# Conv taps read through a DRAM copy of u, and transposes moved from the DMA queues to TensorE, in a hybrid encoder layer

## What is computed

```python
proj = x @ w_in
glu_in, q, k, v, q_mem, gate_logits = split(proj)
a, g = split(glu_in)
u = a * sigmoid(g)                                  # (S, 512)
y_conv = silu(layer_norm(depthwise_conv(u, 31) + dw_b)) @ w_conv_out
y_attn = windowed_gqa(q, k, v, rel_bias, sink) @ w_attn_out   # 8 heads of 64, keys within 128
y_mem = memory_attention(q_mem, mem, w_mem_kv) @ w_mem_out    # 4 heads of 128, 256 keys
gates = sigmoid(gate_logits + b_gate)
merged = gates[0] * y_conv + gates[1] * y_attn + gates[2] * y_mem
x1 = layer_norm(alpha * x + merged @ w_o)
out = layer_norm(alpha * x1 + (silu(x1 @ w_gate) * (x1 @ w_up)) @ w_ffn_out)
```

## Time and profile before

| | |
|---|---|
| three runs | 1162.78, 1255.37, 1316.87 us; median 1255.37 |
| profiled execution | 1163.56 us |
| its slowest core, first to last instruction | 1161.7 us |
| all cores | 1131.6 to 1161.7 us |
| TensorE busy on the slowest core | 1001.5 us (86%) |
| VectorE, ScalarE, GpSimd busy | 403.0, 344.2, 138.0 us |

### The profile page before, as it was taken

The page is one execution under the profiler, slowest core; times in us unless marked ns, Lnnn a source line. Parts: engine busy times, 40 slices in busy tenths (PEclk is TensorE's granted clock), DMA queues, the critical chain, the costliest instruction groups (busy, mean ns, idle before and its releaser), DMA issues.

```text
span 1161.7 us, 15497 instructions; the slowest of 8 cores (1131.6 to 1161.7 us)
## 1 busy us (share of the span) xinstructions
PE 1001.5 (86%) x5526; PEld 456.1 (39%) x5526; DVE 403.0 (35%) x756; ACT 344.2 (30%) x499; POOL 138.0 (12%) x181
## 2 busy tenths in 40 slices
PE   4993995486787399999999874799999999999996
PEld 1441442243333144444444331344444444444442
DVE  1331362352755022222235742334311522251224
ACT  1141563262644022222222463522211211121111
POOL 2200000110113043433330010000000000000000
PEclk9996998897989699999999998899999999999998
DMA  9996112753213689760039599961542144215401
GB/s 136 167 185 107 38 49 62 125 70 74 54 29 59 100 138 180 116 111 1 1 80 277 120 153 131 130 179 55 169 158 91 70 166 152 84 75 179 145 1 72
DMA packets 76042, 124.60 MB, mean 107 GB/s; under 512 B 42240, under 2 KB 52104, under 8 KB 74720
## 3 DMA queue, kind: packets, MB, share of 16 engines
q0 software_dynamic: 13408, 49.55, 24.9%
q1 hardware_dynamic: 45664, 69.87, 21.2%
q10 hardware_dynamic: 16896, 4.20, 5.6%
HBM read 138.32 MB, written 19.93 MB: 136 GB/s over the span
## 4 chain that ended last, share of the span: by engine, by line
PE 71%; DMA 9%; SPq 8%; issue 4%; DVE 3%; ACT 2%; ACTq 1%; POOL 0%; DVEq 0%; POOLq 0%
PE ps L229 71%; SPq L144 7%; DMA arena<-arena 7%; DMA arena<-w_bf_cache 2%; DMA arena<-xt 1%; ACTq L279 1%; DVE arena L1004 1%; DVE arena L1006 1%; ACT arena L1049 1%; SPq L279 1%; DVE arena L589 0%; ACT arena L596 0%; ACT arena L1083 0%; DVE arena L647 0%; DVE arena L675 0%
## 5 line engine op out<-in xcount | busy, mean ns | idle before, releaser
L229 PE MATMUL ps<-arena 128*128 128x512 bf16 (+5 forms) x5372 | 994.7, 368 | 149.5 <-DMA arena<-arena 62.3
L229 PEld LDWEIGHTS ps<-arena 128*128 128x128 bf16 (+2 forms) x5372 | 451.4, 100 | 691.3 <-issue 218.1
L1085 DVE TENSOR_TENSOR arena<-ps,arena 128x512 bf16<-128x512 f32 x88 | 59.7, 690 | 210.1 <-PE ps L229 169.5
L813 DVE SCALAR_TENSOR_TENSOR arena<-arena,ps 128x512 f32<-128x512 f32 x96 | 65.8, 686 | 176.7 <-PE ps L229 172.4
L792 ACT ACTIVATE arena<-ps,bgate_sb 128x512 f32<-128x512 f32 x96 | 65.9, 687 | 189.2 <-PE ps L229 189.2
L1083 ACT ACTIVATE arena<-ps 128x512 f32<-128x512 f32 x88 | 51.3, 597 | 176.4 <-PE ps L229 174.3
L983 ACT ACTIVATE arena<-arena 128x1024 bf16<-128x1024 f32 (+1 forms) x32 | 33.8, 1056 | 152.6 <-DVE arena L1106 128.7
L820 POOL TENSOR_TENSOR arena<-arena 128x512 f32<-128x512 f32 x32 | 41.0, 1283 | 192.7 <-DVE arena L813 192.7
L144 POOL DMA_DIRECT2D out<-arena x16 | 8.5, 532 | 416.3 <-DVE arena L1006 416.3
L644 ACT ACTIVATE arena<-ps 128x1024 bf16<-128x1024 f32 x46 | 46.4, 1023 | 34.1 <-PE ps L229 34.0
L825 POOL TENSOR_TENSOR arena<-arena 128x512 bf16<-128x512 f32 x32 | 40.9, 1277 | 55.9 <-DVE arena L813 48.2
(11 more groups left out here) (81 smaller groups left out, 294.1 us busy)
## 6 DMA issues: line engine op xcount, KB each, us to landing
arena<-w_bf_cache SPq DMA_DIRECT2D x88, 512.0 KB, 3.3
arena<-arena SPq DMA_DIRECT2D x256, 33.8 KB, 1.9
arena<-x SPq DMA_DIRECT2D x16, 512.0 KB, 25.7
out<-arena POOLq DMA_DIRECT2D x16, 512.0 KB, 2.9
arena<-w_f POOLq DMA_DIRECT2D x22, 256.0 KB, 16.3
arena<-w_g POOLq DMA_DIRECT2D x9, 512.0 KB, 12.7
arena<-xt POOLq DMA_DIRECT2D x8, 512.0 KB, 30.5
w_bf_cache<-w_f POOLq DMA_DIRECT2D x8, 512.0 KB, 54.6
```

The costliest lines, as they stand in the source:

```text
L229: return pe.run(lambda: nc.tensor.matmul(out, lhsT, rhs, start=start, stop=stop), deps, inc)
L813: t_y = dve.run(lambda: nc.vector.scalar_tensor_tensor(out=gb[r], in0=gb[r], scalar=1.0, in1=ps[:, bk, :], op0=ALU.add, op1=ALU.mult), [tk ...
L1085: t_a = dve.run(lambda: nc.vector.tensor_tensor(out=actT[:, j, :], in0=ps[:, bU, :], in1=sgf[sr], op=ALU.mult), [tU, t_s, e_state["dep"]])
```

## The change

Three parts. (1) Each piece of u is also stored to DRAM (`u_scratch`) as soon as it exists, on SyncE's queue, and a conv unit's buffer is filled by 4 loads from there, one per shift r, each with 128 runs of 540 elements; the loads wait for the stores of the neighbouring pieces. (2) `w_T` and `m_T` become four TensorE transposes into one single PSUM bank and a copy out of it (VectorE for windowed attention; ScalarE and VectorE in turn, two to one, for memory attention). They are no longer called one piece after the product but are queues `t` and `u` of their own, and `ORDER` is a new string. (3) `d_T` becomes eight TensorE transposes (`d_Tpe`) and a ScalarE copy out of PSUM (`d_Tev`), called two chains later, so that the loop makes two more chains, and the first FFN step stands behind eleven chains instead of ten.

```diff
 ORDER = (
-    "wwawawawkwaawwawawawaawawawwmaacmwacmcmawkmcwawamcwwamcwawawamwcwackcwkcawaccamaakmacaaccmawacaw"
+    "wawawaawwawaaaawawaawwktamwawamwtwwcmwaawuamcwtwkcwakwcmawcmmamcwawawcautwccamcuaacutkwtwawmacmam"
...
+    u_d = nc.dram_tensor("u_scratch", [128, 4, T + 48], BF16, kind="Internal")
...
-    UQ = [[V(143 + 4.25 * i + 1.0625 * j, [128, 544]) for j in range(4)] for i in range(3)]
+    UQr = [V(143 + 4.25 * i, [128, 4, 544]) for i in range(3)]
...
         th_free[r] = [t_u[k, c]]
+        u_store(k, c)
         uq_pump()
...
+    def u_store(k, c):
+        lo = 512 * k + (32 if k else 0)
+        hi = 512 * k + (544 if k < 3 else UW - 512 * 3)
+        ud_tok[k, c] = dma(sp, u_d.ap()[:, c, lo:hi], U0[:, c, lo:hi], ud_slot[4 * k + c], [t_u[k, c], t_pads])
...
     def uq_issue(i):
         k, c = cunits[i]
         r3 = i % 3
-        deps = [t_u[k, c], t_pads, uq_free[r3], btab["st"], btab["cw"]]
-        if k > 0:
-            deps.append(t_u[k - 1, c])
-        if k < 3:
-            deps.append(t_u[k + 1, c])
-        for j in range(4):
-            for r in range(4):
-                lo = 32 + 512 * k - 15 + r
-                uq_tok[i] = dma(sp, UQ[r3][j][32 * r:32 * r + 32, 0:540], U0[32 * j:32 * j + 32, c, lo:lo + 540],
-                                uq_slot[r3], deps)
+        deps = [uq_free[r3], btab["st"], btab["cw"]] + [ud_tok[kk, c] for kk in range(max(k - 1, 0), min(k + 2, 4))]
+        for r in range(4):
+            lo = 32 + 512 * k - 15 + r
+            src = bass.AP(u_d, c * UW + lo, [[4 * UW, 32], [32 * 4 * UW, 4], [1, 540]])
+            uq_tok[i] = dma(sp, UQr[r3][32 * r:32 * r + 32, :, 0:540], src, uq_slot[r3], deps)
...
-    def w_T(n, t_o):
+    def w_T(n):
+        b, dd = banks.alloc(1)
         r = n % 2
-        t_oT[n] = dma_t(sp, qT[:, :, n * 128:(n + 1) * 128], otm[r].rearrange("p a b c -> p (a b c)"), wt_slot[r], [t_o])
-        otm_free[r] = [t_oT[n]]
+        t_o = wst.pop(("V", n))
+        of = otm[r].rearrange("p a b c -> p (a b c)")
+        for c4 in range(4):
+            t_tr = pe.run(lambda: nc.tensor.transpose(
+                psb[:, b, c4 * 128:(c4 + 1) * 128], of[:, c4 * 128:(c4 + 1) * 128], ident_bf[:]),
+                [t_o, dd, t_ident] if c4 == 0 else (), inc=(c4 == 3))
+        otm_free[r] = [t_tr]
+        src = psb[:, b, 0:512].rearrange("p (a b) -> p a b", a=4)
+        t_oT[n] = dve.run(lambda: nc.vector.tensor_copy(qT[:, :, n * 128:(n + 1) * 128], src), [t_tr])
+        banks.release(b, t_oT[n])
...
-    def m_T(u, t_o):
+    def m_T(u):
...
+        om_free[r] = [t_tr]
+        t_omT[u] = evac(qmT[:, h, tt * 512:(tt + 1) * 512], psb[:, b, 0:512], [t_tr])
+        banks.release(b, t_omT[u])
...
-    def d_T(tb):
+    def d_Tpe(tb):
         r = tb % 3
-        t_x1T[tb] = dma_t(act, x1T[:, :, tb * 128:(tb + 1) * 128], x1b[r], xt_slot[r], [d_state.pop(("cb", tb))])
-        x1b_free[r] = [t_x1T[tb]]
+        t_cb = d_state.pop(("cb", tb))
+        bT, dT = banks.alloc(1)
+        for kc in range(8):
+            t_tr = pe.run(lambda: nc.tensor.transpose(
+                psb[:, bT, kc * 128:(kc + 1) * 128], x1b[r][:, kc * 128:(kc + 1) * 128], ident_bf[:]),
+                [t_cb, dT] if kc == 0 else (), inc=(kc == 7))
+        x1b_free[r] = [t_tr]
+        d_state["tr", tb] = (bT, t_tr)
+
+    def d_Tev(tb):
+        bT, t_tr = d_state.pop(("tr", tb))
+        t_x1T[tb] = act.run(lambda: nc.scalar.copy(
+            x1T[:, :, tb * 128:(tb + 1) * 128], psb[:, bT, :].rearrange("p (a b) -> p a b", a=8)), [t_tr])
+        banks.release(bT, t_x1T[tb])
...
+        if 0 <= k - 2 < 16:
+            d_Tpe(k - 2)
         if k + 2 < 16:
             d_S(k + 2)
-        if k >= 0:
+        if 0 <= k - 2 < 16:
+            d_Tev(k - 2)
+        if 0 <= k < 16:
             d_C(k)
...
-        if k >= 0:
-            d_T(k)
...
-    while chain["k"] < 16:
+    while chain["k"] < 16 + 2:
         d_chain()
-        if chain["k"] > 5:
+        if chain["k"] > 6 + 2:
             e_step(si)
```

More of the change, by code:

```diff
@@ L87 @@
 ORDER = (
[L88 to L90 removed]
+    "wawawaawwawaaaawaawawwktamwawamtwwcmwaawuamcwtwkcwakwcmawcmmamcwawawcautwccamcuaacutkwtwawmacmam"
+    "wkuwaccwcacwamckcawwatwctwwacaagwaucwwacccaogmagggkgcmoagacawgmccamtamgagcwoumcucwwcatwumcgacaka"
+    "wgcwmcauccawwacatmacaaawwaawacctcwwcacmctwaccaawaamwamcwaummuaccmactuawaamwacccaaaawaacatwbmauwm"
+    "aamtaauauaaaaaaaa"
 )
@@ L275, in _build @@
     t_small = dma(sp, esink8[:], sinkp_d.partition_broadcast(128).rearrange("p a b -> p (a b)"), s_small)
[L277 to L281, removed]
     def load(out, in_, deps=(), e=None, name="ld"):
@@ L476, in _build @@
     uq_pend = []
+    ud_slot = [new_slot("ud") for _ in range(16)]
+    ud_tok = {}
+    def u_store(k, c):
+        lo = 512 * k + (32 if k else 0)
+        hi = 512 * k + (544 if k < 3 else UW - 512 * 3)
+        ud_tok[k, c] = dma(sp, u_d.ap()[:, c, lo:hi], U0[:, c, lo:hi], ud_slot[4 * k + c], [t_u[k, c], t_pads])
     def uq_load(i):
@@ L653, in w_V @@
         res = wst["S", n]
+        assert otm_free[n % 2] is not None
         b, dd = banks.alloc(2)
@@ L676, in w_V @@
         banks.release(b, t_o, 2)
-        later(1, lambda: w_T(n, t_o))
-    wt_slot = [new_slot("wt") for _ in range(2)]
-    def w_T(n, t_o):
+        wst["V", n] = t_o
+        otm_free[r] = None
+    def w_T(n):
+        b, dd = banks.alloc(1)
         r = n % 2
-        t_oT[n] = dma_t(sp, qT[:, :, n * 128:(n + 1) * 128], otm[r].rearrange("p a b c -> p (a b c)"), wt_slot[r], [t_o])
-        otm_free[r] = [t_oT[n]]
+        t_o = wst.pop(("V", n))
[8 more added lines that the diff above has]
+        banks.release(b, t_oT[n])
     def w_steps(n):
@@ L721, in m_V @@
         t_e = mst.pop(("S", u))
+        assert om_free[r] is not None
         b, dd = banks.alloc(2)
@@ L739, in m_V @@
         banks.release(b, t_o, 2)
-        later(1, lambda: m_T(u, t_o))
-    mt_slot = [new_slot("mt") for _ in range(2)]
-    def m_T(u, t_o):
+        mst["V", u] = t_o
+        om_free[r] = None
+    def m_T(u):
         tt, h = munits[u]
         r = u % 2
-        t_omT[u] = dma_t(sp, qmT[:, h, tt * 512:(tt + 1) * 512].rearrange("p (a b) -> p a b", a=4),
-                         omtm[r].rearrange("p a b -> p (a b)"), mt_slot[r], [t_o])
-        om_free[r] = [t_omT[u]]
+        t_o = mst.pop(("V", u))
+        b, dd = banks.alloc(1)
+        for tbl in range(4):
+            t_tr = pe.run(lambda: nc.tensor.transpose(
+                psb[:, b, tbl * 128:(tbl + 1) * 128], omtm[r][:, tbl, :], ident_bf[:]),
+                [t_o, dd, t_ident] if tbl == 0 else (), inc=(tbl == 3))
+        om_free[r] = [t_tr]
+        t_omT[u] = evac(qmT[:, h, tt * 512:(tt + 1) * 512], psb[:, b, 0:512], [t_tr])
+        banks.release(b, t_omT[u])
     mdn = nc.alloc_sbuf_tensor("mdn", [128, 2, 4], F32)
@@ L911, in _build @@
              qm_list(2) + qm_list(3) + c_main(0, 0) + c_main(0, 1) + c_main(0, 2) + c_main(0, 3))
-    in_order(ORDER, a=mains, w=cat(W), m=cat(M), c=cat(CV), g=[wg_drip(b, i) for b in range(3) for i in range(4)],
+    in_order(ORDER, a=mains, w=cat(W), m=cat(M), t=[(0.3, lambda n=n: w_T(n)) for n in range(16)],
+             u=[(0.3, lambda u=u: m_T(u)) for u in range(16)], c=cat(CV), g=[wg_drip(b, i) for b in range(3) for i in range(4)],
              o=[wos_drip(b) for b in range(3)], b=[(1.0, load_b)], k=[(1.0, lambda: cache_w1(1))] * 8)
@@ L1050, in d_C @@
         d_state["ln"] = t_ln
-    xt_slot = [new_slot("x1t") for _ in range(3)]
-    def d_T(tb):
+    def d_Tpe(tb):
         r = tb % 3
-        t_x1T[tb] = dma_t(act, x1T[:, :, tb * 128:(tb + 1) * 128], x1b[r], xt_slot[r], [d_state.pop(("cb", tb))])
-        x1b_free[r] = [t_x1T[tb]]
+        t_cb = d_state.pop(("cb", tb))
+        bT, dT = banks.alloc(1)
+        for kc in range(8):
+            t_tr = pe.run(lambda: nc.tensor.transpose(
+                psb[:, bT, kc * 128:(kc + 1) * 128], x1b[r][:, kc * 128:(kc + 1) * 128], ident_bf[:]),
[7 more added lines that the diff above has]
+        banks.release(bT, t_x1T[tb])
     sg_free = [[], []]
```

2 lines of the change are left out of this document (1 added, 1 removed).

## The result

The changed kernel took 1061.24 us (median of four executions, 1059.45 to 1079.33). Against the kernel before on the same chip the ratio is 0.9128, with a 95% interval from 0.9098 to 0.9158: 8.7% faster. Executions in which one die is late at a lower clock, or which lie over 1.5% above the fastest of the same kernel, are left out of every ratio and of the medians of the experiments: of the kernel before 1161.13 and 1162.78 us are left, of the changed kernel three, with a median of 1060.53. The forecast was 1057, 4.2 us under the median of all four.

A forecast was written before the change was run, and what follows sets the result against it. The prediction took TensorE to bound the kernel, its idle time and slow clock in two stretches being winnable; from a 1161.7 us span its terms summed to 1055.1, plus 1.9 outside the span: 1057 us, range 1035 to 1095.

The forecast's parts named there:

- Conv copies, +6: New waits for shifted copies: 4 us at conv units 1 and 2, 1 each at 11 and 15; old waits, −37.1, gone.
- The transposes' reason: Stage one's three transpose gaps, 59.6 us, came from SyncE's queue, where transposes start behind a unit's 16 copies.
- Clock, −11.7: Stage one's slow stretches cost 13.7 us at half clock; without the long gaps 2 (0 to 6) remain.
- Transposes on TensorE: 57 ns each: 128 in stage one +7.3 us, 40 before the first FFN step +2.3, the other 88 in gaps, +0.
- Engines in stage one, +5: Copies out of PSUM load VectorE and ScalarE, about 60% busy each, and hold PSUM banks: +5 us, bounds 0 and 25.
- Second stretch: Merged output to first FFN steps: −23.8 us of idle and slow clock blamed on DMA transposes, +5 for a later FFN.
- three signs of being wrong: TensorE idling over 20 us on VectorE or ScalarE; u loads landing after over 9 us; slowest core trailing by 25.
- Late copies, mild: Rival, chance 0.10: bursts of GpSimd's loads cost four exposed conv units 5 to 6 us each, total 1080 us.
- Slower: Rival, chance 0.02: loads through DRAM land late everywhere, units 3, 7, 11 and 15 lose about 40 us each, 1217 us.
- VectorE or ScalarE bounds stage one: Rival, chance 0.10: the engine wait reaches 25 us, not 5, plus 5 for banks in the second stretch, 1082 us.
- The second stretch stays: Rival, chance 0.08: the slowest core's 23.8 us come from slow w1 and w2 loads, left unchanged, 1081 us.
- Transposes at their latency: Rival, chance 0.04: TensorE transposes take 219 ns each, 1086 us, or 1149 if the clock also falls at each place.

The follow-up runs named there:

- Experiments 2: Changed kernel with part 1 alone undone, so 16 copies inside SBUF per conv unit again: 1073.15 us, ratio 0.9218.
- 4: Changed kernel with GpSimd's early w1 cache copies each waiting until TensorE reaches their place: 1047.15 us, ratio 0.9002; timed again 1045.92 beside the changed kernel's 1061.96.
- (3): Changed kernel with part 2 alone undone, so attention outputs transposed by DMA on SyncE's queue again: 1092.33 us, ratio 0.9385.
- (6): Changed kernel with attention transposes by DMA again and GpSimd's early w1 cache copies waiting for TensorE's place: 1074.37 us, ratio 0.9298.
- experiment 7: Changed kernel with the first FFN step one chain earlier: 1059.40 us, ratio 0.9159.
- (1): Changed kernel with part 3 alone undone, x1 transposed by DMA on ScalarE's queue again: 1064.44 to 1089.21 us in four executions, ratio 0.9196 from two.
- 8 to 11: Stage-one transposes done twice: on the changed kernel 1062.78 us; with late w1 cache copies 1048.84, beside bases of 1045.92 (late copies alone) and 1061.96 (changed kernel).

## Why the prediction came close, and where it failed

Span is idle time, time lost to the slow clock (half of TensorE's busy time at 0.50) and work at full clock. By the rows above and the earlier trace rows, in us:

| | before | forecast | after |
|---|---|---|---|
| idle | 1161.7 − 1001.5 = 160.2 | −102.8 | 1059.0 − 1000.8 = 58.2 (−102.0) |
| slow clock | (27.40 + 16.46)/2 = 21.9 | −18.4 | (10.56 + 3.37)/2 = 7.0 (−14.9) |
| work | 979.6 | +14.6 | 993.8 (+14.2) |
| sum | | −106.6 | −102.7 |

(The forecast for idle is its terms less 5.0, and for work plus 5.0, for the 88 transposes that it let fall into gaps.)

*Conv copies, +6: the step that failed.* "0 to 10 us, I take 4" for units 1 and 2, and 1 each for 11 and 15. Measured 11.97 at unit 1 and none at 2, 2.41 at 11 and none at 15: 14.4 in all. I took the landing of 35 to 49 us from the earlier trace rows as what the new loads would meet. TensorE's earlier arrival, 5 to 15 us, was right: it stood ready for unit 1 at 111.4 us, where it had come to it at some 120. But the loads landed later than the copies had, after 62.3 us instead of 44.0: six cache copies stood ahead of them (70.3 us to landing), and the two queues' packets went in turns, 132 and 131. (The Trainium skill's "DMA: Bandwidth & Descriptors", section "Queues, rings and completion order", has this as a rule: each DMA engine goes round the queues packet by packet. The trace agrees, and the forecast left it out.) On the other cores unit 1 waited 7.53 to 12.37 us. Experiments 2 and 4 show the cause, the burst of GpSimd's copies and the way through DRAM together, and 4 its size: 13.4 us with its clock, 16.0 where both were timed side by side.

*The transposes' reason, half wrong.* −59.6 came true, but "The reason is SyncE's queue" holds only for the 15.71 us gap and for some third of the conv waits (26.1 of 37.1 stay without transposes in it). The 18.64 and 25.26 us gaps return, as 23.24 and 26.83, without a unit's 16 copies in that queue (3), and the first of them goes when GpSimd's copies stand back (6). The sum didn't mind, since TensorE takes all 32 away from queue and burst alike. (The landing of up to 32.7 us was read from all 48 transposes; SyncE's own 32 took up to 32.1.)

*Clock, −11.7: too large.* I left 2 us in stage one; three slow stretches lose 10.56/2 = 5.3. They lie at the three waits for loads, of 11.97, 2.41 and 2.50 us, as in the earlier trace rows: what is wrong with the waits is wrong here again.

*Transposes on TensorE: right in price.* (0.61 − 0.22)/7 = 56 ns in the row of eight, and 56 in the doubled run, where 57 was forecast. On the path they seem to cost less than the +7.3: doubling them cost 0.8 to 2.9. The Trainium skill's "TensorE: Matmul & The Clock Gate", section "Part 4: PE-mode transpose", gives about 275 ns; a lone one took 219, and for rows of four and eight the runs don't bear it out. No slow stretch begins at a row of transposes that had not waited.

*Engines in stage one, +5.* Idle there is 21.1; without the conv waits and the 2.50 for output weights 4.2 are left, as before (100.8 − 96.7 = 4.1). So VectorE and ScalarE cost nothing; the "0 to 5 us" that were "held in the engine waits" for the weights were the whole of it.

*Second stretch: too pessimistic, by 8.8 us.* Forecast idle time 34.5 − 17.1 + 5 − 5.0 = 17.4, measured 8.6. The +5 for the later FFN was too much: 4.45 us do stand there, but only four Silu waits follow. By experiment 7 an earlier start pays 7.3 in seven, so the later one costs 1.3. The other 12.4 was the fastest core's idle time of before (17.4, of it 15.3 in nine waits for Silus and 2.0 for VectorE) less 5.0, where 7.3 would have been right. That these 8.8 us nearly cancel the 8.4 of the conv copies is luck: the forecast is closer than its terms.

*The start, put at nothing: 3.5 us.* In its first 60 us TensorE is idle for 60 − 41.96 = 18.0 us, and before for 60 − 45.42 = 14.6. The wait there is for x, 12.5 to 16.9 us from core to core of this one execution, so this is put down to scatter and not to the change; no run tries it. The misses add up: +8.4 conv, +3.5 clock, −2.4 engines, −0.4 work, −8.8 second stretch and +3.5 here make 3.8 of the 3.9 us between the two sums.

*What would show it.* No gap over 5 us: wrong at unit 1. The interleaved part is some 81 us shorter (79.7 idle, 8.4 clock, less 7.3); with the start's 3.5 what follows it comes 77 us earlier (the last gate on ScalarE at 518.5 instead of 595.4 us), not 95. Slow clock at the ends alone: wrong. Unit 11 under 2 us: 2.41. Transposes 57 ns apart, Silu pairs 8.7 us apart (8.60), cores within 15 (13.6): right. None of the three signs of being wrong came: the loads beside units 7, 11 and 15 landed after at most 6.4 us.

*The rivals.* "Late copies, mild" was right that a burst of GpSimd's loads meets the new loads, but it met one unit for 12 us and not four for 5 to 6. "Slower" had landings as late as the earlier trace rows, but they too stayed at one place: the loads issued from 130 us on landed after 3.0 (median of 48). "VectorE or ScalarE bounds stage one" fell with the 4.2 us left. "The second stretch stays" fell: idle time there is 7.9 to 8.8 us on all eight cores with the same weight loads, and a wait for w1 of 7.35 comes back with the DMA transposes (1). "Transposes at their latency" fell with 8 to 11.

## What to carry to other kernels

Before a late transfer is put down to the queue that issued it, look at what the other queues have in flight: here small packets that took turns with large ones landed late, and holding back a prefetch that nothing needed for long, until TensorE reached its place, gave 13 to 16 us. Undo parts of a change alone and together: here they cost 44 us one by one and 67 in one run, and the difference was the price of sharing an in-order queue. Ask of a wait before a loop that other engines pace what the loop would give back: here 8.6 us of waits became 7.3.
